# The fractions of the S5 rotation angles: from GpSimd to VectorE, one operation behind the skip matrix

## The reference

```python
def step(carry, u_i):
    cr, ci = carry
    bu_re = jnp.einsum('bcgh,gph->bcgp', u_i, bb_re)
    bu_im = jnp.einsum('bcgh,gph->bcgp', u_i, bb_im)
    acum_r, acum_i, x_r, x_i = lax.associative_scan(_linrec_combine, (a_r, a_i, bu_re, bu_im), axis=1)
    ...
    y = jnp.einsum('bcgp,ghp->bcgh', x_r, c_re) - jnp.einsum('bcgp,ghp->bcgh', x_i, c_im)
```

## Time and profile before

| | before |
|---|---|
| median of 3 runs | 1462.95 us |
| profiled execution | 1459.49 us |
| its span, first to last instruction | 1457.7 us |
| TensorE matmul busy in the span | 1357.5 us (93%) |
| VectorE busy | 636.1 us (44%) |
| ScalarE busy | 282.7 us (19%) |
| GpSimd busy | 259.3 us (18%) |
| mean granted TensorE clock | 0.980 |

### The profile page before, as it was taken

How to read it: one execution, slowest core, us unless ns; L and a number is a source line. 1 busy time by engine, 2 the same in 40 slices (tenths; PEclk the granted TensorE clock), 3 DMA queues, 4 the chain that set the end, 5 groups by cost and what they waited for, 6 DMA issues and landing times. The chain is left out here.

```text
span 1457.7 us, 24354 instructions
## 1 busy us (share of the span) xinstructions
PE 1357.5 (93%) x10107; PEld 1020.4 (70%) x10107; DVE 636.1 (44%) x1172; ACT 282.7 (19%) x637; POOL 259.3 (18%) x243
## 2 busy tenths in 40 slices
PE   5999999999888986887799999999999999999998
PEld 2476556666556654645368788888888888888887
DVE  2545533100100110010534327376299999986563
ACT  2223121110100110010111032110244444320000
POOL 0000100000000000000365540099333343000000
PEclk9999999999998999999999999999999999999999
DMA  9855769999999999999743343556564444333440
GB/s 398 326 232 212 298 267 403 426 426 427 424 426 426 424 426 424 425 426 426 269 156 116 129 160 122 196 180 216 193 214 171 169 161 163 131 146 143 173 172 31
DMA packets 50826, 388.21 MB, mean 266 GB/s; under 512 B 6288, under 2 KB 21392, under 8 KB 29088
## 3 DMA queue, kind: packets, MB, share of 16 engines
q1 hardware_dynamic: 48128, 381.35, 65.5%
q10 hardware_dynamic: 2592, 5.31, 1.0%
HBM read 379.76 MB, written 6.88 MB: 265 GB/s over the span
## 5 line engine op out<-in xcount | busy, mean ns | idle before, releaser
L1490 DVE TENSOR_TENSOR ada_part<-ada_part,ps 64x256 f32<-64x256 f32 x32 | 13.5, 423 | 418.1 <-ACT ada_part L1445 418.1
L2590 PE MATMUL ps<-hT,ring 128*128 128x256 f32 x768 | 174.3, 383 | 1.0 <-PEq L2029 1.0
L2590 PEld LDWEIGHTS ps<-hT,ring 128*128 128x128 f32 x768 | 143.3, 190 | 24.5 <-issue 4.3
L1558 POOL TENSOR_SCALAR end_stat<-end_ss 128x1 f32<-128x1 f32 x2 | 0.9, 472 | 492.2 <-ACT expert L1548 492.2
L1445 ACT ACTIVATE ada_part<-ps 64x256 f32<-64x256 f32 x32 | 12.1, 377 | 326.5 <-PE ps L1395 326.5
L1358 PE MATMUL ps<-memT,hT 128*128 128x256 f32 x192 | 54.8, 449 | 17.5 <-DMA hT<-in_mem_quarters 16.7
L267 PE MATMUL ps<-ring,hT 128*128 128x512 f32 x160 | 69.8, 593 | 0.0
L1061 PEld LDWEIGHTS ps<-sel,tokens 128*128 128x128 f32 x544 | 62.0, 192 | 8.0 <-issue 8.0
L1878 PE MATMUL ps<-ring,zT 128*128 128x256 f32 x288 | 66.8, 379 | 0.0
L1061 PE MATMUL ps<-sel,tokens 128*128 128x64 f32 x544 | 64.3, 276 | 0.7 <-DVE sel L1070 0.7
L1358 PEld LDWEIGHTS ps<-memT,hT 128*128 128x128 f32 x192 | 42.9, 229 | 27.2 <-DMA hT<-in_mem_quarters 18.6
(11 more groups left out here) (654 smaller groups left out, 2558.1 us busy)
## 6 DMA issues: line engine op xcount, KB each, us to landing
ring<-in_weights SPq DMA_DIRECT2D x69, 2048.0 KB, 8.1
expert<-in_experts SPq DMA_DIRECT2D x36, 2048.0 KB, 23.8
ring<-in_experts SPq DMA_DIRECT2D x35, 2048.0 KB, 23.6
expert_room<-in_experts SPq DMA_DIRECT2D x12, 2048.0 KB, 22.5
late_room<-in_experts SPq DMA_DIRECT2D x12, 2048.0 KB, 23.9
hT<-in_mem_quarters SPq DMA_DIRECT2D x20, 512.0 KB, 22.8
s_c_bar<-c_bar_out ACTq DMA_DIRECT2D x16, 256.0 KB, 2.6
c_bar<-s_c_bar SPq DMA_DIRECT2D x16, 256.0 KB, 2.8
```

The costliest lines, as they stand in the source:

```text
L1490: dve.tensor_tensor(act_s, gate, h_ps[w3_out, :], ALU.mult).then_inc(act_ready, 1)
L2590: last = pe.matmul(out[:, f, :], w[:, kk, (2 * h + f) * P:(2 * h + f + 1) * P], k.hT[:, kk, :], start=(kk == 0), stop=(kk == KD - 1))
```

## The change

The function `fraction` and its calls leave GpSimd. VectorE runs it: `fraction(0)` ahead of the loop, `fraction(q + 1)` in step q right behind the skip matrix. Operands, semaphores and all other instructions stay.

```diff
             @block.gpsimd
             def _(pool):
-                def fraction(q):
-                    b = q % 2
-                    pool.wait_ge(angle_ready, q + 1)
-                    pool.tensor_tensor(sin[b][:], cos[b][:], sin[b][:], ALU.subtract).then_inc(frac_ready, 1)
-
-                fraction(0)
                 for q in range(N):
-                    if q >= 2:
-                        fraction(q - 1)
                     if q:
                         pool.wait_ge(bu_done, q)
...
-                fraction(N - 1)
 
             @block.vector
             def _(dve):
+                def fraction(q):
+                    b = q % 2
+                    dve.wait_ge(angle_ready, q + 1)
+                    dve.tensor_tensor(sin[b][:], cos[b][:], sin[b][:], ALU.subtract).then_inc(frac_ready, 1)
+
...
                 dve.memset(x_im[:, :, :, 0:1], 0.0)
+                fraction(0)
                 dve.wait_ge(own_in, 16)
...
                     dve.tensor_tensor(skip[:, b, :], skip_ps, own[:], ALU.mult).then_inc(bu_used, 1)
+                    if q < N - 1:
+                        fraction(q + 1)
                     dve.drain()
```

## The result

The changed kernel is slower: 1468.88 us median (7 runs, 1466.34 to 1471.37) against 1462.45 us of the kernel before (7 runs beside them, 1459.17 to 1464.43). The ratio is 1.0052 with a 95% interval of 1.0039 to 1.0064, that is +5.7 to +9.4 us; the two medians themselves lie 6.4 us apart. The forecast was 1469.5, with 1466.3 to 1472.5 as range.

What follows compares the result with a forecast made beforehand. The prediction took VectorE and TensorE as both full, the later one ending the stage. +9.1 - 3.3 + 1.3 = +7.1 us on VectorE, less TensorE's 0.45, gave +6.6 us: 1469.5 us, range 1466.3 to 1472.5.

Steps and rivals of the forecast that it cites:

- Two engines full, `y` the link, 0.45 us between them: In the stage, VectorE and TensorE are both full; `y(q)` needs VectorE's last sum; TensorE ends later by 0.45 us.
- Fractions on VectorE, +9.1: In VectorE's loop, 15 added fractions at 0.61 us each lengthen the chain by 9.1 us; `fraction(0)` is free.
- The upper bound, a pause of 0.16 us at each fraction's wait: On VectorE, each of 15 fractions might cost 0.77 us including a pause, 11.5 us in all.
- The 26 us that VectorE seemed to have spare: VectorE's apparent spare time in the stage, read as its late start of 15.6 us and pauses of 2.4 us.
- Fractions off GpSimd, -3.3: On VectorE, four sums lengthened by fractions running on GpSimd become short again, winning 3.3 us.
- over 1.1 us each: Time each of 15 GpSimd fractions would block VectorE if all excluded it, some 17 us; the rows show four.
- The sets, +1.3 in 0 to 1.8: GpSimd's 13 sets of products in steps 1 to 13 cost VectorE 1.37 us each, 1.3 us more than before.
- the forecast 13.2 to 13.4 us: Length of VectorE's steps in the profile after, regular, in place of 12.2 to 13.9 us.
- Sum: VectorE's chain grows by 7.1 us; TensorE absorbs 0.45 us at the end, leaving +6.6 us.
- The clock: Rival, 3%: TensorE's granted clock falls behind its three or so pauses, about 1 us staying each time, +3 us, 1472.5.
- The pause forecast ahead of `y(15)`: TensorE's idle time ahead of `y` at step 15 in the profile after, under 1 us.
- Late angles: Rival, 5%: VectorE waits 0.4 us for ScalarE's angles in at most 5 of 15 steps, +1.9 us, 1471.4.

Runs made afterwards that it cites:

- e3: The kernel before without the fraction (cos - sin left out, a constant written by the rounding step): 1460.74 us, ratio 0.9991 to the kernel before.
- e2: The kernel before with one more 128 x 512 subtraction on VectorE in steps 0 to 14, fractions still on GpSimd: 1471.27 us, ratio 1.0060.
- e5: The kernel before with only the odd-numbered 8 of 16 fractions moved to VectorE: 1464.80 us, ratio 1.0018.
- e8: The changed kernel with the fraction behind the scans in place of behind the skip matrix: 1468.30 us, ratio 1.0050 to the kernel before.
- e1: The changed kernel with GpSimd's sets of products waiting for `rotated`: 1461.50 us, ratio 0.9990 to the kernel before.

## Why the prediction was right, point by point

- *Two engines full, `y` the link, 0.45 us between them*: right. e3 shows TensorE alone: its own work ends 0.60 us ahead of `y(15)` of the kernel before. With VectorE later (e2, e5, e8) `y(15)` starts 0.10 to 0.11 us behind the sum.
- *Fractions on VectorE, +9.1*: right, 15 x 0.61 by step 14 of the profile after. The upper bound, a pause of 0.16 us at each fraction's wait, did not come: in step 0 the fraction starts 0.20 us behind the start of the skip matrix, and the next sum 0.77 us behind the fraction where it had started 0.37 us behind the skip matrix. The 26 us that VectorE seemed to have spare were read a little wrong: the late start (15.6) and the pauses at the heads (2.4) make 18; about 6 more are the gaps of some 0.1 us behind the drains, with the one pause in step 12, and the rest lies behind its last sum. The conclusion stands: each added fraction lengthened a step by its full 0.61 us.
- *Fractions off GpSimd, -3.3*: right; no L2737 or L2738 in the 16 steps is longer than 0.70 us. One fraction met a set instead (0.95 us in step 1). The prediction's "over 1.1 us each" for a blocked operation is a little high: the largest that the rows show is 1.08.
- *The sets, +1.3 in 0 to 1.8*: at the upper end. Steps 1 to 13 take 1247.73 - 1074.50 = 173.23 us, 13 x 11.92 = 154.96 of it undisturbed, so 18.3 us, +1.8. This is the term that was mis-sized, by 0.5 us, and the price per set is not the reason. Of the 18.3 us, 0.27 belong to the fraction that met a set, and 0.35 to the one pause in step 12; what is left is 17.6, 1.36 per set, and I had read 1.37 from step 9. The kernel before has that pause too, in its step 12, and I had counted it among the sets: theirs were 16.2 us, not 16.5. Steps 1 and 12, where these two lie, are also the ones outside the forecast 13.2 to 13.4 us (13.55 and 13.61). The pause before, and after:

```profile
1221.57 0.69 DVE L2752 TENSOR_TENSOR s_x_re<-s_x_re,s_t_re 128x512 f32<-128x512 f32 x1 [0.48 <-issue]
```

```profile
1225.92 0.42 DVE L2742 TENSOR_TENSOR_SCAN s_z_re<-s_decay,s_z_re 128x128 f32<-128x128 f32 x1 [0.42 <-issue]
```

- *Sum*: 9.1 - 3.3 + 1.8 = 7.6 for the chain (measured 7.58; the forecast was 7.1), less 0.45, plus 0.64 of the clock, makes 7.8 (measured 7.78). The 0.64 is itself read from `y(15)`, so this closes the account and doesn't prove it.
- *The clock* was a rival at 3%, with 1 us each time. It did come, once in three pauses, so the chance was set too low. The price was of the wrong form: I let 1 us stay for each fall, but in e2 and e8 the clock fell behind the first and the second pause, and TensorE had made up its delay by the next one; at the end it waited for VectorE, 0.73 and 0.82 us. Only the fall behind the last long pause left something, 0.64 us. The pause forecast ahead of `y(15)` was missing in the profile after for the same reason.
- *Late angles*: not with the changed kernel, as argued. Where TensorE is the later engine (e1), they are late in 5 steps, which is the condition that the prediction named.
- *TensorE covers it*: refuted by e2 and e5; each operation counts.

The forecast's 6.6 us and the measured 7.6 (5.7 to 9.4) differ by 1.0. In the profiles the difference is 1.2, the sets' 0.5 and the clock's 0.6; the interval is too wide to tell these from the medians.

## What to carry to other kernels

When the busiest engine is 99.7% busy and another "only" 88%, look at whether the second one ever waits inside the loop. If it doesn't, it may be full too, and a pause of the busiest engine ahead of what needs the second one's result (here 0.27 us ahead of `y(8)`) shows that it sets the pace there. Work that is moved onto such an engine costs its whole time there, less what it had cost that engine from its old place (here 9.1 less 3.3 us). An operation that is 1.9 times shorter on the new engine (0.68 us against 1.27) still loses when the old one had time. If an operation on GpSimd slows VectorE, moving it in time, beside operations with an operand in PSUM, can win more than moving it to VectorE: here one wait ahead of the sets took away what 16 operations had cost. It won nothing clear over the kernel before, since TensorE's own work ends only 0.6 us earlier.

## What was not expected of the hardware

The exclusion between GpSimd and VectorE holds for scans too. In step 9 of the changed kernel a set begins under the scans:

```profile
1187.43 1.71 POOL L2700 TENSOR_TENSOR ab_tmp<-b_raw,s_a_rows 128x256 f32<-128x256 f32 x2 [8.88 <-PE ps L2603]
```

```profile
1187.41 0.40 DVE L2743 TENSOR_TENSOR_SCAN s_z_im<-s_decay,s_z_im 128x128 f32<-128x128 f32 x1
1187.73 0.89 DVE L2742 TENSOR_TENSOR_SCAN s_z_re<-s_decay,s_z_re 128x128 f32<-128x128 f32 x1
1188.54 0.88 DVE L2743 TENSOR_TENSOR_SCAN s_z_im<-s_decay,s_z_im 128x128 f32<-128x128 f32 x1
```

Two scans of 0.40 us take 0.89 and 0.88. The Trainium skill (SBUF — State Buffer, section "Who interferes with whom") gives this for VectorE instructions with two SBUF inputs in general; the scan, whose decay is a column read over and over, behaves so here.

TensorE's clock fell behind some pauses and not behind others that were hardly shorter, or no shorter. e2 and e8 show it behind one pause each:

```profile
1127.74 0.72 PE L2625 MATMUL ps<-uT,skip 128*128 128x128 f32 x2 [2.21 <-issue]
```

```profile
1127.70:1129.70 2.00, 1.96 (x30) 1.67 (x33) 1.84 (x4) 1.93 (x6) 0.13 (x1) 0.52 0.00 0
1129.70:1131.70 2.00, 2.00 (x17) 1.42 (x10) 1.93 (x5) 1.03 (x3) 1.15 (x1) 0.62 0.15 16
```

```profile
1178.39 0.47 PE L2624 MATMUL ps<-uT,skip 128*128 128x128 f32 x2 [2.64 <-issue]
```

```profile
1178.40:1180.40 2.00, 2.00 (x35) 1.49 (x35) 1.84 (x4) 1.68 (x5) 0.00 (x0) 0.68 0.07 17
1180.40:1182.40 2.00, 2.00 (x8) 1.64 (x6) 1.91 (x5) 0.00 (x0) 0.00 (x0) 0.50 0.35 91
```

It fell behind pauses of 2.21 (e2), 2.35 (changed) and 2.64 us (e8), and stayed at 1.00 behind those of 1.57 and 2.11 us in the changed kernel, 1.62 and 2.11 in e2, 2.12 in e8 and behind one of 2.5 us elsewhere in the program. What decides between them stays open. In e8 it cost nothing at the end: `y(15)` waits for VectorE there, whose chain goes on at its pace during a slow stretch of TensorE (the three steps behind it take 13.3 us each), and the next pause is shorter for it (0.33 us at `y(12)` in e8, where the changed kernel has 2.35). In e2 too `y(15)` waits for VectorE; whether TensorE's lag behind the fall led a fraction to meet the added operation in step 6, for 0.6 us, isn't shown.
